# The S5 stage of a two-layer encoder: other engines for the first tables, another loop order, and output-projection splits moved under the last gate unit

## The chip, the cores and the metric

One core of a Trainium2 chip runs the whole program in one launch. The time is device microseconds, the median of three executions. The engines are TensorE (PE in the profile; PEld is its weight load), VectorE (DVE), ScalarE (ACT), GpSimd (POOL) and SyncE (SP), which here issues all the large transfers. Each runs its own list of instructions in order, and they wait for one another through semaphores.

## What is computed

Two layers on a sequence of 1024 tokens of width 1024, batch 1, in float32. Layer 0 mixes with S5 (the stage that the change touches), layer 1 with HGRN2; after each mixer come a projection, a layer norm, a SwiGLU feed-forward of hidden width 2816 and another layer norm.

```python
def s5_direction(u, lam_re, lam_im, log_step, b_re, b_im, c_re, c_im):
    ...
    lam_dt = lam * step
    lam_bar = jnp.exp(lam_dt)
    b_bar = ((lam_bar - 1.0) / lam)[..., None] * b
    powers = jnp.exp(lam_dt[None] * jnp.arange(1, blk + 1, dtype=f32)[:, None, None])
    ...
        bu = jnp.einsum('lbgh,gph->lbgp', u_blk.astype(jnp.complex64), b_bar)
        _, h_loc = lax.associative_scan(combine, (a_blk, bu), axis=0)
        h_all = h_loc + powers[:, None] * h[None]
        y = jnp.einsum('ghp,lbgp->lbgh', c, h_all).real
    ...

def s5_mixer(x, w_in, lam_re, lam_im, log_step, b_re, b_im, c_re, c_im, d_skip, w_glu, b_glu, w_out):
    u = x @ w_in
    ...
    y = (y_fw + y_bw) + d_skip * u
    y = jax.nn.gelu(y)
    y = y * jax.nn.sigmoid(y @ w_glu + b_glu)
    return y @ w_out
```

There are 64 groups of 16 channels with 64 complex states each, scanned over the sequence in both directions.

## The kernel before

All of S5 is in `s5_gate_block`: five instruction lists written out by hand, one per engine. The channels are worked in 8 blocks of 128 (the index `n`, `KT` = 8). Each float32 operand of a large product is split in two rounded parts (`hi` by ScalarE, `lo` = rest by VectorE or GpSimd), and a product is three TensorE instructions. The sequence is cut in chunks of `L` = 8 tokens.

**The front.** x is transposed in 16 tiles (`turn_x`, `split_x`). Meanwhile VectorE works out the tables: `tables_to_first_power` (lambda-bar; 11 small instructions after ScalarE's tanh and sin), `tables_to_input_factors`, then the input factors `b_bar` of block 0, then `make_bl` (12 products of 128x512, of which GpSimd takes the 6 of the backward side), then `scan_factors` (six levels of `k.mu`, ended by the semaphore `mu`), then `scan(0)`.

**Block n.** `inputs(n)` on TensorE makes u = x @ w_in for 128 channels, 48 instructions in two halves; it needs `w_hi` and `w_lo`, of which there is one buffer each: ScalarE's `split_w(n)` waits until `inputs(n-1)` is through (`u_done`), GpSimd's `split_w(n)` follows it (`w_lo_done`). `make_bl` fills `bl`; `turn_bl` transposes it (16 instructions) and ScalarE's `keep_min` puts it in `s5_min`; `start_state` multiplies u of each chunk by it; `scan` on VectorE runs over the chunks in PSUM; `keep_state` on ScalarE copies the result. `make_cl` (backward side, GpSimd, 6 products) and `make_cl_in_psum` (forward side, VectorE, 12 smaller ones, from a copy of c that ScalarE's `place_c` puts in PSUM) fill `cl` for the output. `make_kern` makes the kernel inside a chunk; ScalarE copies it, `turned_diagonal` on VectorE adds the skip term, and SyncE regroups it by way of DRAM (`place_toeplitz`). `within_chunks` and `across_chunks` then give y, `keep_y` copies it, and SyncE regroups it by way of DRAM.

**The loop** (n = 1 to 7) on the three engines that matter:

- TensorE: `start_state(n)`, `make_kern(n)`, `within_chunks(n-1)`, `across_chunks(n-1)`, `inputs(n+2)` (only n = 2 to 5), `turn_bl(n+1)`.
- ScalarE: `keep_kern_rows(n)`, `keep_y(n-1)`, `keep_u(n+2)`, `split_w(n+3)`, `place_b`, `keep_min(n+1)`, `place_c(n+1)`, `keep_state(n)`, `gelu(n-1)`.
- GpSimd: `make_cl(n)`, `ins(n+1)` (its `b_bar` and its `bl`), `split_w(n+3)` (n up to 4). Each item waits for what it reads and overwrites.

SyncE runs one list too: `regroup_u(n+1)`, `put_y` and `regroup_y(n-1)`, then `place_toeplitz(n)`; so the kernel of block 1 is placed only after y of block 0 has been stored.

**The end of S5.** Eight gate units (y @ w_glu, 48 instructions each, two halves) end in `gates(n)`: a sigmoid on ScalarE and a multiplication on VectorE (`mixed`). Then `project_and_feed` begins as a new block of instructions: the gated rows and the pieces of w_out are split on ScalarE and VectorE, and TensorE begins the output projection when row 0 and quarter 0 of piece 0 are split.

Of the kernel before, what the change touches and what calls it, by code (L numbers as in the profile page):

```python
# [78 lines left out]

class Core:  # L80
# [34 lines left out]
    def sb(self, name, shape, dt=F32, keep=False):  # L115
        if dt == F32R:
            with self.nc.sbuf_tensor(name + "_plain", shape, F32) as self.plain[name]:
                pass
        return (self.ctx if keep else self.areas[-1]).enter_context(self.nc.sbuf_tensor(name, shape, dt))
# [42 lines left out]
PIECE = 2 * D  # L162
SLOTS = 6


def out_projection_block(k, tag, w, residual, natural, gamma=None, beta=None):

    k.projection = (tag, w, residual, natural)
    if not natural:
        k.first, k.hi0, k.lo0 = (k.sb("w_" + n, [P, PIECE], F32R, keep=True) for n in ("raw0", "hi0", "lo0"))  # L170
# [24 lines left out]
def project_and_feed(k, gamma_out, beta_out, first_weights=(), spill=None, out=None):  # L195
# [29 lines left out]
    PAIRS = NT // 2  # L225
    turns = out is None
# [179 lines left out]
    with nc.Block() as block:  # L406
        @block.sync
        def _(s):
# [54 lines left out]
            s.wait_ge(S["w_lo"], 2 * KT)  # L463
# [71 lines left out]
        def _(t):  # L535
# [156 lines left out]
            for n, (dh, kh) in enumerate(PIECES):  # L692
                if n < 2:
                    for at in range(4):
                        t.wait_ge(S["x_lo"], at + 1)
                        t.wait_ge(S["w_lo"], 4 * n + at + 1)
                        for tt in range(4):
                            project(n, at, tt, 2 * tt + dh)
                else:
                    t.wait_ge(S["x_lo"], KT)  # L700
                    t.wait_ge(S["w_lo"], 4 * n + 4)
# [45 lines left out]
        def _(a):  # L747
# [3 lines left out]
            def split_piece(n, at):  # L751
# [3 lines left out]
                if n == 2 and at == 0:  # L755
# [94 lines left out]
            for n in range(2):  # L850
                for at in range(4):
                    if not natural or n and at == 3:
                        split_x(4 * n + at)
                    if n or not natural:
                        split_piece(n, at)
# [74 lines left out]
        def _(v):  # L930
            chain = Steps(S["chain"])

            def split_x(kk):
                if not natural:
                    v.wait_ge(S["x_hi"], kk + 1)
# [5 lines left out]
            def split_piece(n, at):  # L941
                dh, kh = PIECES[n]
                if n or not natural:
                    v.wait_ge(S["w_hi"], 4 * n + at + 1 - (4 if natural else 0))
# [202 lines left out]
            for n in range(2):  # L1147
                for at in range(4):
                    split_x(4 * n + at)
                    split_piece(n, at)  # L1150
# [203 lines left out]
def s5_gate_block(k, w_glu):  # L1354
# [5 lines left out]

    w_raw = k.sb("s5_w_raw", [P, KT, P])
# [4 lines left out]
    b_pair = k.sb("s5_b_pair", [P, 2, DP, 2, GRP])  # L1366
# [41 lines left out]
        "u_kept", "bar", "bl", "bl_bw", "pow", "cl", "b_placed", "kern_done", "kern_rows_kept",  # L1408
        "kern_rows_done", "kern_out", "toep_placed", "u_out", "u_grouped", "bl_turned", "min_kept", "in_done",
        "scan", "pads", "state_kept", "toep_done", "out_done", "y_kept", "y_out", "y_ungrouped", "y_done", "mu", "cl_fw", "c_placed", "diag",  # L1410
        "y_hi", "y_lo", "y_lo_last", "glu_loaded0", "glu_loaded1", "glu_hi0", "glu_hi1", "glu_lo0", "glu_lo1", "unit", "gated", "mixed", "early")}
# [7 lines left out]
    FIRST_POWER = LAM_READY + GJ - 1 + 11  # L1419
    POW = 18  # L1420
# [41 lines left out]
    def make_bl(e, n, sides=(0, 1), sem="bl", temp=None):  # L1462
        link = Steps(S[sem], n and n * BL - BL // 2)
        for d in sides:
# [5 lines left out]
            product_steps(link, e, b, pows, [bl[:, q, dps] for q in range(2)],  # L1470
                          gen_t[:, :, 0:L, :] if temp is None else temp)
# [13 lines left out]
    def make_cl_in_psum(e, n):  # L1485
        link = Steps(S["cl_fw"], (n - 1) * CLF)
# [7 lines left out]
    with nc.Block() as block:  # L1494
        @block.sync
        def _(s):
# [139 lines left out]
            s.wait_ge(S["early"], 16)  # L1636

        @block.tensor
        def _(t):
# [50 lines left out]
            def turn_bl(n):  # L1690
                if n >= 1:
                    t.wait_ge(S["bl"], (n + 1) * BL - BL // 2)
# [4 lines left out]
                else:  # L1697
                    t.wait_ge(S["kern_rows_done"], n)
                    t.wait_ge(S["cl_fw"], (n - 1) * CLF)
                for m in range(4):  # L1700
                    if n == 0:
                        t.wait_ge(S["bl" if m < 2 else "bl_bw"], BL // 4 * (m % 2 + 1))
# [92 lines left out]
            inputs(2, (0, 1))  # L1795
            start_state(1)
            make_kern(0)
            inputs(3, (0, 1))
            for n in range(1, KT):
# [4 lines left out]
                across_chunks(n - 1)  # L1804
                if 2 <= n < KT - 2:
                    inputs(n + 2, (0, 1))
                if n < KT - 1:
                    turn_bl(n + 1)

            def gate_part(n, halves, kks):  # L1810
                for half in halves:
# [9 lines left out]
                    if kks[-1] == KT - 1:  # L1821
                        ins.then_inc(S["unit"], 1)

# [1207 lines left out]
```

## Time and profile before

| | us |
|---|---|
| median of 3 executions | 2645.22 (2644.72 to 2647.85) |
| the profiled execution, its own time | 2644.07 |
| its span in the trace | 2642.3 |
| S5 stage (last gate multiplication begins) | 407.43 |

TensorE is busy 94% of the span, but in the S5 stage less: in the windows of 50 us from 100 to 350 it was busy 31.0, 41.8, 41.9, 32.7 and 45.4. The rest of the program (feed-forwards, HGRN2) has no line in the change, apart from counts. Times in rows are microseconds from the start of the span, "idle before" is how long the engine stood before an instruction, and the name behind the arrow is what ended that.

### The profile page before, as it was taken

To read this page: it belongs to the slowest core of one execution; us is meant where nothing else is said; L and a number is where in the kernel's file an instruction comes from. 1 tells how busy PE (TensorE), PEld (TensorE's weight loads), DVE (VectorE), ACT (ScalarE), POOL (GpSimd) and SP (SyncE) were. 2 spreads that over 40 slices of the span, in tenths; PEclk is the share of its full clock that TensorE was granted. 3 is DMA by queue.
4 is the path that set the end of the run, shared out by engine and by line. 5 is a ranking of instruction groups with operands and counts; after the bars stand their busy time and mean duration, and the time that the engine had idled before them with its cause. 6 is when DMAs were issued, how large, how long until landed. Compare 5 with 4: busy or idle time off the path is not lost. (4 is left out here: it accounts for less than half of the span.)

```text
span 2642.3 us, 39850 instructions
## 1 busy us (share of the span) xinstructions
PE 2488.7 (94%) x12860; PEld 2085.5 (79%) x12860; DVE 1920.4 (73%) x3122; ACT 900.0 (34%) x1455; POOL 727.2 (28%) x557
## 2 busy tenths in 40 slices
PE   7678799999999999999999999998799999999997
PEld 6567687878888878887888888887677888887886
DVE  8879826777877758884667666676586777785887
ACT  3223324243333335523322223223124333333641
POOL 6768810243333310001111111112024333331000
PEclk9888899999999999999999999999899999999999
DMA  4143314056677678722010110100404667667863
GB/s 146 56 118 105 97 56 160 13 150 214 192 222 214 204 264 281 233 102 63 25 41 24 40 32 24 40 24 16 159 8 135 203 207 220 209 200 259 296 207 130
DMA packets 442288, 355.97 MB, mean 135 GB/s; under 512 B 30272, under 2 KB 376512, under 8 KB 438464
## 3 DMA queue, kind: packets, MB, share of 16 engines
q1 hardware_dynamic: 442176, 354.52, 42.9%
q8 instruction: 65, 1.06, 0.2%
q14 instruction: 47, 0.39, 0.0%
HBM read 296.31 MB, written 58.13 MB: 134 GB/s over the span
## 5 line engine op out<-in xcount | busy, mean ns | idle before, releaser
L2514 PE MATMUL ps<-aT_hi,w_hi 128*128 128x512 f32 x624 | 250.7, 402 | 3.8 <-DVE hg_q_raw L2793 2.0
L2464 POOL TENSOR_TENSOR w_lo<-w_raw_plain,w_hi 128x1024 fp32r<-128x1024 f32 x38 | 90.9, 2401 | 575.3 <-ACT w_hi L62 575.3
L2514 PE MATMUL ps<-aT_hi,w_lo 128*128 128x512 f32 x624 | 245.2, 393 | 0.0
L2514 PE MATMUL ps<-aT_lo,w_hi 128*128 128x512 f32 x624 | 243.8, 391 | 0.0
L616 PE MATMUL ps<-aT_hi,hgo_w_sets 128*128 128x512 f32 x640 | 203.0, 393 | 0.0
L616 PE MATMUL ps<-aT_hi,s5o_w_sets 128*128 128x512 f32 x640 | 202.7, 393 | 0.0
L1284 POOL TENSOR_TENSOR s5o_w_sets_plain<-s5o_w_sets_plain 128x512 f32<-128x512 f32 x80 | 109.9, 1374 | 216.7 <-DMA s5o_w_sets_plain<-in_ffn_w_in_dram 216.7
L1284 POOL TENSOR_TENSOR hgo_w_sets_plain<-hgo_w_sets_plain 128x512 f32<-128x512 f32 x80 | 110.6, 1383 | 212.8 <-DMA hgo_w_sets_plain<-in_ffn_w_in_dram 212.8
L616 PEld LDWEIGHTS ps<-aT_hi,hgo_w_sets 128*128 128x128 f32 x640 | 120.4, 188 | 26.4
L616 PEld LDWEIGHTS ps<-aT_hi,s5o_w_sets 128*128 128x128 f32 x640 | 120.2, 188 | 26.3
L2514 PEld LDWEIGHTS ps<-aT_hi,w_hi 128*128 128x128 f32 x624 | 117.5, 188 | 26.9 <-DVE hg_q_raw L2793 2.4
L2514 PEld LDWEIGHTS ps<-aT_hi,w_lo 128*128 128x128 f32 x624 | 117.1, 188 | 25.5
L2514 PEld LDWEIGHTS ps<-aT_lo,w_hi 128*128 128x128 f32 x624 | 117.5, 188 | 23.6
L666 PE MATMUL ps<-aT_hi 128*128 128x512 f32 x576 | 133.0, 390 | 0.0
L62 ACT ACTIVATE s5o_w_sets<-s5o_w_sets_plain 128x512 fp32r<-128x512 f32 (+1 forms) x153 | 101.7, 682 | 90.1 <-POOL s5o_w_sets_plain L1284 53.0
L2554 PE MATMUL ps<-hg_q_decayed,hg_k_used 128*128 128x128 f32 x896 | 121.3, 291 | 11.0 <-DVE hg_q_decayed L2859 11.0
L62 ACT ACTIVATE hgo_w_sets<-hgo_w_sets_plain 128x512 fp32r<-128x512 f32 (+1 forms) x153 | 101.4, 682 | 88.2 <-POOL hgo_w_sets_plain L1284 52.4
L2554 PEld LDWEIGHTS ps<-hg_q_decayed,hg_k_used 128*128 128x128 f32 x896 | 117.2, 197 | 16.9 <-DVE hg_q_decayed L2859 12.4
L666 PEld LDWEIGHTS ps<-aT_hi 128*128 128x128 f32 x576 | 108.1, 188 | 22.9
L616 PE MATMUL ps<-aT_lo,s5o_w_sets 128*128 128x512 f32 x320 | 124.4, 389 | 0.0
L616 PE MATMUL ps<-aT_lo,hgo_w_sets 128*128 128x512 f32 x320 | 124.3, 389 | 0.0
L2859 DVE TENSOR_TENSOR hg_q_decayed<-hg_q_decayed,hg_gate_totals 128x512 f32<-128x512 f32 x96 | 76.2, 835 | 65.2 <-PE ps L2554 65.2
(445 smaller groups left out, 6246.9 us busy)
## 6 DMA issues: line engine op xcount, KB each, us to landing
s5o_w_sets_plain<-in_ffn_w_in_dram SPq DMA_DIRECT2D x168, 256.0 KB, 3.2
hgo_w_sets_plain<-in_ffn_w_in_dram SPq DMA_DIRECT2D x168, 256.0 KB, 3.3
w_raw_plain<-in_hg_w_in_dram SPq DMA_DIRECT2D x40, 512.0 KB, 3.9
aT_hi_plain<-in_ffn_w_out_dram SPq DMA_DIRECT2D x64, 256.0 KB, 4.6
s5o_w_sets_plain<-in_ffn_w_in_dram SPq DMA_DIRECT2D x96, 128.0 KB, 2.7
hgo_w_sets_plain<-in_ffn_w_in_dram SPq DMA_DIRECT2D x96, 128.0 KB, 2.8
s5o_hidden<-s5o_home_plain SPq DMA_DIRECT2D x11, 1024.0 KB, 7.0
hgo_hidden<-hgo_home_plain SPq DMA_DIRECT2D x11, 1024.0 KB, 6.8
```

The lines of the kernel that those rows point to most:

```text
L62: return eng.activation(hi, src, ACT.Copy)
L616: ins = t.matmul(ps[:, 4 * second + to, :], w[:, kk, :], x_sets[x][xs][:, kk, :], start=(kk == 0 and m == 0), stop=(kk == 3 and m == 2))
L666: ins = t.matmul(ps[:, out_bank(p, tt), :], x[:, rows], w, start=(j == 0 and m == 0), stop=(j == LAST and m == 2))
L1284: g.tensor_tensor(other, one, other, PRODUCTS[r][2]).then_inc(S["set_sum"], 1)
L2464: g.tensor_tensor(w_lo[b][:, :, :], w_raw[b][:, :, :], w_hi[b][:, :, :].bitcast(F32), ALU.subtract).then_inc(E[f"w_lo_done{b}"], 1)
L2514: ins = t.matmul(ps[:, half, :], w[b][:, kk, :], x[:, kk, cols], start=(kk == 0 and q == 0), stop=(kk == KT - 1 and q == 2))
L2554: ins = t.matmul(bank_rows(2 + 2 * (lv % 2))[:, c, :], k_used[lv % 2][:, c * HC:(c + 1) * HC], q_used(lv, c), start=True, stop=True)
L2859: ins = v.tensor_tensor(qs, qs, bc(pair(d, lv, d), 2, [P, T // (2 << lv), 1 << lv]), ALU.mult)
```

## The change

- **First tables.** VectorE keeps 4 of the 11 instructions (`tables_to_inverse`) and waits for the tanh alone; the other 7 become 8 on GpSimd (`first_power`) ahead of `later_powers`. `make_bl` of block 0 is all VectorE's. GpSimd then waits for `mu`, so that it runs beside neither that nor `scan_factors`, and only then does `split_w(1)` and `ins(1)`. The forward `cl` of block 0 moves from GpSimd to VectorE (`make_cl_in_psum(0)`, behind `scan(0)`).
- **Before the loop.** `start_state(1)` moves between the halves of `inputs(2)`; on ScalarE `keep_state(0)` stands before the second half's copy.
- **The loop.** On TensorE `turn_bl(n+1)` comes before `inputs(n+2)`; on ScalarE `keep_u(n+2)` and `split_w(n+3)` follow `place_c(n+1)`. On VectorE `turned_diagonal(n)` comes right behind the first level of the scan. GpSimd's order in the loop is as before.
- **The end.** The last gate unit runs by contraction block, both halves of a block together. Under it ScalarE and VectorE split piece 0 of w_out and, as TensorE lets go of each row (`row_free`), rows 0 to 3 of y; the output projection no longer splits or awaits these. `w_raw0` and `w_hi0` are placed on tables that S5 has finished with.

```diff
             def turn_bl(n):
                 if n >= 1:
-                    t.wait_ge(S["bl"], (n + 1) * BL - BL // 2)
+                    t.wait_ge(S["bl"], (n + 1) * BL)
...
             def make_kern(n):
-                t.wait_ge(S["cl"], (n + 2) * CLS)
-                t.wait_ge(S["cl_fw"], (n or 1) * CLF if n < KT - 1 else (n - 1) * CLF + CLS)
+                t.wait_ge(S["cl"], (n + 1) * CLS)
+                t.wait_ge(S["cl_fw"], ((n or 1) + 1) * CLF if n < KT - 1 else n * CLF + CLS)
...
             turn_bl(1)
-            inputs(2, (0, 1))
+            inputs(2, (0,))
             start_state(1)
+            inputs(2, (1,))
             make_kern(0)
             inputs(3, (0, 1))
...
                 within_chunks(n - 1)
                 across_chunks(n - 1)
+                if n < KT - 1:
+                    turn_bl(n + 1)
                 if 2 <= n < KT - 2:
                     inputs(n + 2, (0, 1))
-                if n < KT - 1:
-                    turn_bl(n + 1)
...
+                else:
+                    t.wait_ge(S["gated"], 2 * (n - 4) + 2)
+                    for kk in range(KT):
+                        gate_part(n, (0, 1), (kk,))
...
             for n in range(KT):
+                if n == KT - 2:
+                    a.wait_ge(S["early"], 16)
+                    a.wait_ge(S["out_done"], KT)
+                    for at in range(4):
+                        split_hi(a, in_four(k.first)[:, at, :], in_four(k.early)[:, at, :]).then_inc(S["next_w_hi"], 1)
+                if n == KT - 1:
+                    for kk in range(FIRST_ROWS):
+                        a.wait_ge(S["row_free"], kk + 1)
+                        a.wait_ge(S["mixed"], 2 * (kk + 1))
+                        split_hi(a, in_tokens(k.aT_hi[:, kk, :]), in_chunks(row(kk))).then_inc(S["next_x_hi"], 1)
                 gates(n)
...
             make_b_bar(v, 0)
             v.wait_ge(S["pow"], POW)
-            make_bl(v, 0, (0,))
+            make_bl(v, 0)
             scan_factors()
...
             scan(0)
+            v.wait_ge(S["c_placed"], 1)
+            make_cl_in_psum(v, 0)
...
             split_w(0)
-            g.wait_ge(S["tab"], FIRST_POWER)
+            first_power()
             later_powers()
-            g.wait_ge(S["bar"], BAR)
-            make_bl(g, 0, (1,), "bl_bw", cl[0][:, 0, 0:PR, 0:L, :])
+            g.wait_ge(S["mu"], 1)
             split_w(1)
-            g.wait_ge(S["bl"], BL // 2)
             ins(1)
+            g.wait_ge(S["c_kept"], 8)
+            make_cl(g, 0, 1, S["cl"], 0)
             split_w(2)
-            g.wait_ge(S["mu"], 1)
-            g.wait_ge(S["c_kept"], 8)
-            make_cl(g, 0, 0, S["cl"], 0)
-            make_cl(g, 0, 1, S["cl"], CLS)
             split_w(3)
```

Where it moves instructions: TensorE in the loop, pass n = 2 before. L1746 is `start_state`, L1722 `make_kern`, L1762 `within_chunks`, L1775 `across_chunks`, L1667 `inputs` (48 rows of which the first two are here), L1707 `turn_bl`.

```order
L1722 MATMUL ps<-s_cl_plain,s_b_pair 32x128 x16
L1762 MATMUL ps<-s_u_grp,s_pw_in 128x128 x8
L1775 MATMUL ps<-s_state,s_cl 128x128 x32
L1667 MATMUL ps<-aT_hi,s_w_hi 128x512
L1667 MATMUL ps<-aT_lo,s_w_hi 128x512
```

The same place of the changed kernel; L1748, L1788, L1801, L1733 and L1693 are the lines 1722, 1762, 1775, 1707 and 1667 of before.

```order
L1748 MATMUL ps<-s_cl_plain,s_b_pair 32x128 x16
L1788 MATMUL ps<-s_u_grp,s_pw_in 128x128 x8
L1801 MATMUL ps<-s_state,s_cl 128x128 x32
L1733 MATMUL ps<-ident,s_bl 128x128 x16
L1693 MATMUL ps<-aT_hi,s_w_hi 128x512
```

The transposes of `bl` now stand ahead of the input product of the same pass; nothing was added.

ScalarE, pass n = 4 before: `keep_y`, `keep_u`, `split_w`, `place_b`, `keep_min`, `place_c`, `keep_state`.

```order
L1917 ACTIVATE h<-ps 128x4x128 x2
L1866 ACTIVATE h<-ps 128x512 x2
L62 ACTIVATE s_w_hi<-s_w_raw 128x1024
L1875 ACTIVATE s_b_pair<-s_b_bar 64x16x16 x2
L1890 ACTIVATE s_min_plain<-ps 128x512 x4
L1881 ACTIVATE ps<-s_c_all 128x128
L1910 ACTIVATE s_state<-ps 128x4x128 x4
```

The same pass of the changed kernel:

```order
L1953 ACTIVATE h<-ps 128x4x128 x2
L1909 ACTIVATE s_b_pair<-s_b_bar 64x16x16 x2
L1926 ACTIVATE s_min_plain<-ps 128x512 x4
L1917 ACTIVATE ps<-s_c_all 128x128
L1900 ACTIVATE h<-ps 128x512 x2
L62 ACTIVATE s_w_hi<-s_w_raw 128x1024
L1946 ACTIVATE s_state<-ps 128x4x128 x4
```

The copy of u and the split of the next weights now stand behind `place_c`, just ahead of `keep_state`.

GpSimd, the end of one pass and the begin of the next in the changed kernel (the same items in the same order as before): `bl` of block 3, the split for block 5, `cl` of block 3.

```order
L1474 TENSOR_TENSOR s_gen_t<-s_b_bar,s_pw 128x4x128
L1476 TENSOR_TENSOR s_bl<-s_bl,s_gen_t 128x512
L2314 TENSOR_TENSOR s_w_lo<-s_w_raw,s_w_hi 128x1024
L1472 TENSOR_TENSOR s_cl<-s_c_all,s_pw 128x576
L1474 TENSOR_TENSOR s_gen_t<-s_c_all,s_pw 128x576
```

The split stands between `bl` of one pass and `cl` of the next, as it did.

## Rows read from the trace of the kernel before

**Rows 1.** The page's part 1: busy time, share of span, instructions.
```profile
PE 2488.7 (94%) x12860; PEld 2085.5 (79%) x12860; DVE 1920.4 (73%) x3122; ACT 900.0 (34%) x1455; POOL 727.2 (28%) x557
```

**Rows 2.** Waits of TensorE, 0 to 420: total us, times, longest.
```profile
PE ps L1746 <- ACT s_state L1910: 26.9, 7, 11.4
PE ps L1818 <- POOL aT_lo L2269: 4.6, 2, 3.6
```

**Rows 3.** Timeline of ScalarE: start, us, line, tiles [idle before <-releaser].
```profile
165.56 0.60 ACT L1866 ACTIVATE h<-ps 128x512 f32<-128x512 f32 x1 [4.91 <-PE ps L1667]
...
228.44 0.60 ACT L1866 ACTIVATE h<-ps 128x512 f32<-128x512 f32 x1 [4.91 <-PE ps L1667]
...
259.65 0.60 ACT L1866 ACTIVATE h<-ps 128x512 f32<-128x512 f32 x1 [4.91 <-PE ps L1667]
...
276.63 1.08 ACT L1917 ACTIVATE h<-ps 128x512 f32<-128x512 f32 x2 [5.33 <-PE ps L1775]
```

**Rows 4.** Timeline of GpSimd, one pass of the loop.
```profile
198.91 2.36 POOL L2259 TENSOR_TENSOR s_w_lo<-s_w_raw,s_w_hi 128x1024 fp32r<-128x1024 f32 x1 [4.87 <-ACT s_w_hi L62]
201.21 1.18 POOL L1446 TENSOR_TENSOR s_cl_plain<-s_c_all,s_pw 128x576 f32<-128x576 f32 x1
...
208.95 0.40 POOL L1446 TENSOR_TENSOR s_b_bar<-s_b_all,s_coef 128x128 f32<-128x128 f32 x1
...
211.71 1.06 POOL L1446 TENSOR_TENSOR s_bl<-s_b_bar,s_pw 128x512 f32<-128x512 f32 x1
...
224.45 1.30 POOL L1450 TENSOR_TENSOR s_bl<-s_bl,s_gen_t 128x512 f32<-128x512 f32 x1
230.13 2.36 POOL L2259 TENSOR_TENSOR s_w_lo<-s_w_raw,s_w_hi 128x1024 fp32r<-128x1024 f32 x1 [4.38 <-ACT s_w_hi L62]
```

**Rows 5.** Timeline of TensorE, two places of the loop.
```profile
217.16 0.47 PE L1667 MATMUL ps<-aT_hi,s_w_hi 128*128 128x512 f32 x1 [1.28 <-ACT h L1917]
...
282.93 3.78 PE L1707 MATMUL ps<-ident,s_bl 128*128 128x128 f32 x16 [6.35 <-issue]
```

**Rows 6.** Timeline of VectorE, the front.
```profile
30.57 0.22 DVE L2097 TENSOR_TENSOR s_cl<-s_cl 128x64 f32<-128x64 f32 x1
...
35.90 0.69 DVE L1446 TENSOR_TENSOR s_bl<-s_b_bar,s_pw 128x512 f32<-128x512 f32 x1
36.51 1.55 DVE L1448 TENSOR_TENSOR s_gen_t<-s_b_bar,s_pw 128x512 f32<-128x512 f32 x1
...
64.56 2.60 DVE L2127 TENSOR_SCALAR s_mu<-s_mu 128x448 f32<-128x448 f32 x1
```

**Rows 7.** Timelines of ScalarE and TensorE, first store of y.
```profile
129.29 1.06 ACT L1917 ACTIVATE h<-ps 128x512 f32<-128x512 f32 x2
...
144.69 2.71 PE L1762 MATMUL ps<-s_u_grp,s_pw_in 128*128 128x128 f32 x11 [8.69 <-DMA s_pw_in<-s_scratch_kern]
```

**Rows 8.** Timelines of VectorE and ScalarE, scan of block 6.
```profile
264.26 0.46 DVE L1446 TENSOR_TENSOR s_cl_plain<-ps,s_pw 128x288 f32<-128x288 f32 x1
...
269.68 0.69 DVE L2159 TENSOR_TENSOR s_scan_t<-ps,s_mu 128x512 f32<-128x512 f32 x1
...
294.50 1.08 ACT L1910 ACTIVATE s_state<-ps 128x512 f32<-128x512 f32 x2 [0.90 <-DVE ps L2167]
```

**Rows 9.** Timeline of GpSimd, first gate weights split.
```profile
296.92 2.38 POOL L2264 TENSOR_TENSOR s_w_lo<-s_w_raw,s_w_hi 128x1024 fp32r<-128x1024 f32 x1
```

**Rows 10.** Timelines of VectorE, ScalarE and TensorE, end of the S5 stage.
```profile
407.43 0.69 DVE L2251 TENSOR_TENSOR h<-h,s_scan_t 128x512 f32<-128x512 f32 x1 [4.80 <-ACT s_scan_t L1950]
...
408.42 2.04 ACT L62 ACTIVATE aT_hi<-h 128x1024 fp32r<-128x1024 f32 x1 [1.02 <-PEq L1494]
...
415.56 2.44 ACT L62 ACTIVATE aT_hi<-h 128x1024 fp32r<-128x1024 f32 x1
...
413.25 0.77 PE L577 MATMUL ps<-w_raw,aT_hi 128*128 128x512 f32 x1 [6.58 <-DVE w_hi L945]
```

**Rows 11.** Windows: us, busy us (x) of PE, PEld, DVE, ACT, POOL, PEclk, DMA.
```profile
282.90:287.00 4.10, 3.78 (x16) 3.06 (x16) 3.83 (x17) 2.05 (x4) 3.94 (x4) 0.56 0.38 112
```

More of the change, by code:

```diff
@@ L169, in out_projection_block @@
     if not natural:
-        k.first, k.hi0, k.lo0 = (k.sb("w_" + n, [P, PIECE], F32R, keep=True) for n in ("raw0", "hi0", "lo0"))
+        k.lo0 = k.sb("w_lo0", [P, PIECE], F32R, keep=True)
         k.raw0 = k.plain["w_raw0"]
@@ L851, in _ @@
                 for at in range(4):
-                    if not natural or n and at == 3:
+                    if (4 * n + at == KT - 1) if natural else (4 * n + at >= ROWS_DONE):
                         split_x(4 * n + at)
-                    if n or not natural:
+                    if n:
                         split_piece(n, at)
@@ L942, in split_piece @@
                 dh, kh = PIECES[n]
-                if n or not natural:
-                    v.wait_ge(S["w_hi"], 4 * n + at + 1 - (4 if natural else 0))
+                if n:
+                    v.wait_ge(S["w_hi"], 4 * n + at + 1 - 4)
                 v.tensor_tensor(in_four(proj_lo[dh][kh])[:, at, :], in_four(raw[n])[:, at, :],
@@ L1359, in s5_gate_block @@
     GA = SG // 2
+    b_pair = k.sb("s5_b_pair", [P, 2, DP, 2, GRP])
+    k.under.close()
+    k.first, k.hi0 = (k.sb("w_" + n, [P, PIECE], F32R, keep=True) for n in ("raw0", "hi0"))
+    k.sb("s5_gap", [P, HALF // 8])
     w_raw = k.sb("s5_w_raw", [P, KT, P])
@@ L1460, in make_b_bar, with make_bl @@
         product_steps(link, e, b, cf, [of(b_bar[:, q, :, :]) for q in range(2)], t)
-    def make_bl(e, n, sides=(0, 1), sem="bl", temp=None):
-        link = Steps(S[sem], n and n * BL - BL // 2)
-        for d in sides:
+    def make_bl(e, n):
+        link = Steps(S["bl"], n * BL)
+        for d in range(2):
             half = [P, PR, L, GRP]
@@ L1469, in make_bl @@
             pows = [bc(asc[:, q, at, L - 1::-1] if d == 0 else asc[:, q, at, 0:L], 3, half) for q in range(2)]
-            product_steps(link, e, b, pows, [bl[:, q, dps] for q in range(2)],
-                          gen_t[:, :, 0:L, :] if temp is None else temp)
+            product_steps(link, e, b, pows, [bl[:, q, dps] for q in range(2)], gen_t[:, :, 0:L, :])
     def powers(n, d, rows_):
@@ L1822, in gate_part @@
                         ins.then_inc(S["unit"], 1)
+                    elif n == KT - 1 and half == 1:
+                        ins.then_inc(S["row_free"], 1)
             t.wait_ge(S["glu_lo0"], 1)
@@ L1981, in _ @@
             keep_min(1)
+            place_c(0)
+            keep_u(2, (0,))
+            keep_state(0)
             place_c(1)
-            keep_u(2)
+            keep_u(2, (1,))
             split_w(3)
-            keep_state(0)
             keep_kern_rows(0)
@@ L2004, in _ @@
                     keep_y(0)
+                if n >= 2 and n + 2 < KT:
+                    keep_u(n + 2)
+                    if n + 3 < KT:
+                        split_w(n + 3)
                 if n == KT - 2:
@@ L2247, in _ @@
             for n in range(KT):
+                if n == KT - 2:
+                    for at in range(4):
+                        v.wait_ge(S["next_w_hi"], at + 1)
+                        v.tensor_tensor(in_four(k.hi0)[:, at, :], in_four(k.early)[:, at, :],
+                                        in_four(k.first)[:, at, :].bitcast(F32), ALU.subtract).then_inc(S["next_lo"], 1)
+                if n == KT - 1:
+                    for kk in range(FIRST_ROWS):
+                        v.wait_ge(S["next_x_hi"], kk + 1)
+                        v.tensor_tensor(in_tokens(k.aT_lo[:, kk, :]), in_chunks(row(kk)),
+                                        in_tokens(k.aT_hi[:, kk, :]).bitcast(F32), ALU.subtract).then_inc(S["next_lo"], 1)
                 for half in range(2):
```

116 lines of the change are left out of this document (72 added, 44 removed).

## Prediction, made before the changed kernel ran

> **What bounds the kernel now.** Read first the busy times: TensorE works 94% of the span [rows 1], so outside the S5 stage nothing can move, and a gain or loss has to come from its idle time in S5. Then the waits of TensorE there [rows 2]: 26.9 us for `keep_state`, that is for VectorE's scans, and 4.6 us for GpSimd's split of y. Then ScalarE's timeline: the second half of `keep_u` begins the moment `inputs` ends, so its rows give the length of a pass. `inputs(4)` ends at 165.56 and `inputs(7)` at 259.65 [rows 3]: three passes in 94.1 us, 31.4 each. Last GpSimd's list [rows 4], which looks harmless: one pass is `split_w` at 198.91, `cl` from 201.21, `b_bar` from 208.95, `bl` from 211.71 until 225.75 (224.45 + 1.30), together 26.8 us, and then it idles 4.38 us until ScalarE has split the next weights. It fits under the 31.4 only because `inputs` runs while `bl` is being made. The reader is to see that these two are what the new loop order puts in series.
>
> **The front.** Three things, followed to the place where the loop takes over.
> First tables: VectorE no longer waits for the sine and has 4 instructions, not 11. I take 3 us off the second half of x's transposes and all that follows them (bounds 0 and 3.5).
> `make_bl(0)`, scan factors: a 128x512 product on VectorE took 0.69 us just before GpSimd's began and 1.55 beside it; a 128x64 product 0.22 alone; the last factor instruction, begun beside GpSimd, 2.60 [rows 6]. GpSimd now stands still until `mu`. So 12 products x 0.7 = 8.4 us instead of the six contended ones, then 6 levels x 4 instructions x 0.22 plus copies and the negation, about 6 us instead of 23. From 32.9 (35.90 less 3): 41.3, then 47.3 for `mu` (bounds 46 and 50), against 67.2 (64.56 + 2.60). So `scan(0)` begins 20 us earlier.
> The Trainium skill (SBUF — State Buffer, Who interferes with whom) has it that a VectorE instruction with two SBUF inputs contends with a GpSimd one that reads SBUF, and the later one is held. The rows above agree; if the slow level were VectorE's own, 12 x 1.5 and 23 us would put `mu` at 74 and the whole result some 26 us later than I forecast.
> But GpSimd has waited too. From 47.3 it needs, by its rows [rows 4], split 2.4, `b_bar` 2.8, `bl` 14.0, `cl` 7.7 and split 2.4: 76.6 before the weights of `inputs(2)` are split. Then, estimated from the rows of the loop: half a product 5.6 and 1.4 for an idle stretch before it; two copies 1.2; `start_state(1)`, paced by four more, 5; the other half 5.6: 95.4. ScalarE's copy and split 1.7, GpSimd's split 2.4, `cl(1)` 7.7, `b_bar` 2.8, `bl(2)` 14.0: 124. `turn_bl(2)` 3.8, then `place_c` and `keep_y(0)`: 129.8, where before it ended at 130.35 (129.29 + 1.06) [rows 7]. From there the order on SyncE is unchanged: y is stored, then the kernel placed, and 14.3 us later `within_chunks(1)` starts [rows 7], so at 144.1; the chunk products, some 8.3 at the low clock, make it 152.4; with `turn_bl(3)` 3.8 and `inputs(4)` 11.3 it is 167.5. Before: 165.56. The 20 us of `scan(0)` have gone in GpSimd's later start: **+1.9 us** (bounds -2 and +5).
>
> **The loop.** Moving `turn_bl(n+1)` ahead of `inputs(n+2)` closes a ring. `turn_bl` needs `bl` from GpSimd; `inputs` stands behind it on TensorE; ScalarE may overwrite the one `w_hi` buffer only when `inputs` is through; GpSimd's `split_w(n+3)` waits for that, and `cl`, `b_bar` and the next `bl` stand behind it in its list. Its price, all from rows: GpSimd 26.8 [rows 4]; 16 transposes 3.8 and 48 products from 217.16 to 228.44 = 11.3 [rows 3, 5]; ScalarE's copy and split until GpSimd starts, 228.44 to 230.13, 1.7 [rows 3, 4]. Together 43.6 us. From `inputs(4)` to `inputs(7)` the ring is closed three times (splits for blocks 5, 6, 7): 3 x 43.6 - 94.1 = **+36.7 us** (bounds: +35 if the transposes need no more than 3.2; +53 if every input product runs half its length at the low clock, 3 x 5.6 more; I take the low end, since the 3.8 was read with the granted clock at 0.56 of full, the low level of 1.2 GHz for most of it, and is paid already [rows 11]). What else the order brings, `place_c` without waiting behind `inputs`, and `turned_diagonal` early, shortens waits that are no longer last. VectorE needs 24.8 + 5.4 us in a pass (scan 6 from 269.68 to 294.47, the forward `cl` before it from 264.26) [rows 8] and now idles 13.
> The Trainium skill (Perfetto Trace Analysis, Optimization Strategy) says that the same gap coming back in each pass can mean that there is no buffer for the next tile. Before, no gap here was of that kind; by that rule the new one would be, since `w_hi` is single.
>
> **Out of the loop.** Before, `inputs(7)` ended at 259.6 and scan 6 34.9 us later, for it was queued behind scan 5 [rows 3, 8]. Now scan 5 is long done: copy, `keep_state(5)`, half of `start_state(6)`, 3 us, and 24.8: 27.8. **-7.0 us** (bounds -5 and -8). GpSimd's last two `cl` (2 x 7.7) begin when `across_chunks(5)` ends. Before, that was 17.0 us after `inputs(7)` (276.63 - 259.65) [rows 3]; without the transposes between, 3.8 and a wait of some 1.5, it is 11.7, so `split_glu(0)` starts 27.1 after it; before it was 296.92 - 259.65 = 37.3 [rows 9], 10.2 more. The stage's tail is 3.2 us nearer to its splits of y than to its scans, and 4.6 us were waited for them [rows 2]: **-3.2 us** (bounds 0 and -4.6).
>
> **The last gate unit and the output projection.** Before, TensorE stood 6.58 us [rows 10] between the stages: sigmoid, multiplication, then row 0 and a quarter piece split. Now it can begin when the new block does. Under the last unit (11 us on TensorE) ScalarE has four row splits of 2.0 to 2.4 and VectorE four of the same size behind them; the first can begin 1.4 us into the unit. The last ends at 1.4 + 4 x 2.3 + 2.6 = 13.2, then two multiplications 1.4: 14.6 against 12.5 before, so the stage ends 2 us later; the block's first instruction comes at 408.42 before, hence TensorE at 410.5 instead of 413.25. With a little less time at the low clock: **-3.5 us** (bounds -5 and +1). The next pieces' splits are done before TensorE reaches them, 11 us on. The four quarter splits of w_out fall in gaps of 4.80 us on ScalarE.
>
> **Sum.** 1.9 + 36.7 - 7.0 - 3.2 - 3.5 = +24.9 us. The profiled execution took 2644.07, 1.8 more than its span of 2642.3, and the median of the runs is 1.2 above it; I put the difference on the median: 2645.2 + 24.9 = 2670.
>
> **The rivals.**
> The ring doesn't bind and VectorE does. Then each pass is 30.2 us, and the early `scan(0)` reaches the end: scan 6 would begin at 47.5 + 6 x 30.2 + 5.4 (the added `cl` of block 0) = 234.1 instead of 269.68 [rows 8], 35.6 us earlier; with the projection's 3.5: 2606. It decides from the point at which `bl` is ready when `across_chunks` ends. For it speaks that VectorE was busy nearly all of a pass before; against it that each link of the ring is a wait in the code. Chance 0.05.
> The ring binds, but the front's gain arrives at `inputs(4)` and the clock costs nothing, some 20 us less than my sum: 2650, still within 0.2% of before. GpSimd's 29 us behind `mu` speak against it. Chance 0.03.
> The ring binds and TensorE, which now idles 10 us twice in a pass, runs the products behind at the low clock: up to 3 x 5.6 more, and 2 in the front: 2689. The stretch of the 16 transposes shows 0.56 of full speed on the mean, so the clock was already rising within it, and little is left for the products. Chance 0.07.
> The splits under the last unit hold up the stage by 5 us more: 2675, inside the range.
>
> **The numbers.** The forecast has 0.85. The ends of its own terms would reach from 2653 to 2700, which they do not do together; 2660 to 2681 leaves out both outer rivals and the far tails, about 2 in 10. About 0.2%, 5 us, is what a measurement of this kernel can tell. Faster 0.05, same 0.03, slower 0.92.
>
> **What would show it.** Right: in the trace of after `keep_u`'s second halves for blocks 4 to 7 some 43 to 44 us apart; `turn_bl` idle about 10 us before each and released by GpSimd's `bl`; `mu` at 46 to 50 and `scan(0)` right behind; GpSimd idle 17 us before each split; TensorE idle below 4 us ahead of the projection. Wrong: passes of 30 to 32 us, or `turn_bl` released by anything but `bl`.

## The result, and the profile after

| | median us | lowest to highest | profiled execution, its span |
|---|---|---|---|
| before | 2645.06 | 2644.72 to 2647.85 (4 runs) | 2644.07, 2642.3 |
| after | 2668.97 | 2666.09 to 2671.44 (4 runs) | 2669.25, 2667.5 |

The changed kernel is slower: 1.009 times the time before (95% interval 1.0076 to 1.0103), 23.9 us by the medians and 25.2 us by the spans. The forecast was 2670. Two executions lie far outside all others (10923 us in run 2, 3514 us for the kernel before beside runs 9 and 10) and are left out of every median below.

Part 1 of the page of after, engine by engine: busy time, share of the span, instructions.

```profile
PE 2495.0 (94%) x12860; PEld 2089.1 (78%) x12860; DVE 1914.2 (72%) x3133; ACT 900.2 (34%) x1456; POOL 714.1 (27%) x553
```

Against [rows 1] TensorE is busy 6.3 us longer with the same 12860 instructions; the other 19 us are idle time. Of the 6.3 us, 6.0 lie in the S5 stage, where the mean granted clock fell from 0.89 to 0.87. Nothing is computed more, so the loss has to be read from waits. TensorE's waits from 0 to 450 us (us in total, times, longest):

```profile
PE ps L1733 <- POOL s_bl L1476: 32.8, 5, 8.3
PE ps L1772 <- ACT s_state L1946: 22.3, 7, 10.6
PE ps L1693 <- POOL s_w_lo L2314: 11.0, 3, 6.3
PE ps L1748 <- POOL s_cl L1476: 9.9, 2, 5.8
PE ps L1788 <- DMA s_pw_in<-s_scratch_kern: 7.5, 1, 7.5
```

L1733 is `turn_bl`, L1748 `make_kern`. In [rows 2] the first place belonged to `keep_state`, that is to VectorE's scans. Now `turn_bl` waits longest, and for GpSimd. ScalarE's timeline shows how far apart the passes lie: `keep_u`'s second halves for blocks 4 to 7 (start, us, line, tiles, idle before and releaser), to be laid beside [rows 3]:

```profile
167.05 0.60 ACT L1900 ACTIVATE h<-ps 128x512 f32<-128x512 f32 x1 [4.90 <-PE ps L1693]
...
210.40 0.60 ACT L1900 ACTIVATE h<-ps 128x512 f32<-128x512 f32 x1 [4.90 <-PE ps L1693]
...
254.21 0.60 ACT L1900 ACTIVATE h<-ps 128x512 f32<-128x512 f32 x1 [4.90 <-PE ps L1693]
...
298.30 0.60 ACT L1900 ACTIVATE h<-ps 128x512 f32<-128x512 f32 x1 [4.89 <-PE ps L1693]
```

The passes take 43.35, 43.81 and 44.09 us; before it was 31.4. The first of them, link by link, in the timelines of GpSimd, TensorE, ScalarE and again GpSimd:

```profile
168.73 2.36 POOL L2314 TENSOR_TENSOR s_w_lo<-s_w_raw,s_w_hi 128x1024 fp32r<-128x1024 f32 x1 [17.09 <-ACT s_w_hi L62]
...
194.14 1.26 POOL L1476 TENSOR_TENSOR s_bl<-s_bl,s_gen_t 128x512 f32<-128x512 f32 x1
```

```profile
195.46 3.83 PE L1733 MATMUL ps<-ident,s_bl 128*128 128x128 f32 x16 [8.26 <-POOL s_bl L1476]
198.94 0.65 PE L1693 MATMUL ps<-aT_hi,s_w_hi 128*128 128x512 f32 x1
```

```profile
210.89 1.05 ACT L62 ACTIVATE s_w_hi<-s_w_raw 128x1024 fp32r<-128x1024 f32 x1
```

```profile
212.08 2.35 POOL L2314 TENSOR_TENSOR s_w_lo<-s_w_raw,s_w_hi 128x1024 fp32r<-128x1024 f32 x1 [16.67 <-ACT s_w_hi L62]
```

From split to split it is 212.08 - 168.73 = 43.35: GpSimd's list until 195.40 (26.7), the transposes until the product starts at 198.94 (3.5), the product until 210.40 (11.5), copy and split on ScalarE (1.7). No link overlaps another. That is what a closed chain (a ring) looks like: each engine idles in each pass, and each waits for the one before it.

At the end of the stage, the timelines of ScalarE, VectorE and TensorE; `aT_hi` and `aT_lo` x4 are the splits of y's rows under the last gate unit, behind the last sigmoid of the unit before it at 424.84, to be laid beside [rows 10] and this sigmoid of before:

```profile
395.72 0.69 ACT L1950 ACTIVATE s_scan_t<-ps,glu_col 128x512 f32<-128x512 f32 x1 [4.80 <-PE ps L1818]
```

After:

```profile
424.84 0.69 ACT L1986 ACTIVATE s_scan_t<-ps,glu_col 128x512 f32<-128x512 f32 x1 [4.80 <-PE ps L1845]
426.21 8.71 ACT L62 ACTIVATE aT_hi<-h 128x1024 fp32r<-128x1024 f32 x4 [0.68 <-PE ps L1845]
435.14 1.38 ACT L1986 ACTIVATE s_scan_t<-ps,glu_col 128x512 f32<-128x512 f32 x2 [0.22 <-PE ps L1845]
```

```profile
428.51 8.73 DVE L2301 TENSOR_TENSOR aT_lo<-h,aT_hi 128x1024 fp32r<-128x1024 f32 x4 [2.25 <-ACT aT_hi L62]
```

```profile
438.76 0.77 PE L586 MATMUL ps<-w_raw,aT_hi 128*128 128x512 f32 x1 [2.96 <-PEq L1519]
```

TensorE stands 2.96 us between the stages instead of 6.58. The projection starts at 438.76, 25.5 us later than before, and that is the whole loss: from there to the end of the span it is 2228.7 us, and before 2229.0.

### The profile page after: what moved, and what is told of

The parts are those of the page before. It is cut to its first block and busy times, and to the rows that moved or that the text cites. A ratio compares the mean times of both kernels' runs of the same rounds, so it can differ in the third digit from the quotient of the medians.

```text
span 2667.5 us, 39858 instructions
## 1 busy us (share of the span) xinstructions
PE 2495.0 (94%) x12860; PEld 2089.1 (78%) x12860; DVE 1914.2 (72%) x3133; ACT 900.2 (34%) x1456; POOL 714.1 (27%) x553
## 3 DMA queue, kind: packets, MB, share of 16 engines
q8 instruction: 65, 1.06, 0.2%
## 5 line engine op out<-in xcount | busy, mean ns | idle before, releaser
L2584 PEld LDWEIGHTS ps<-aT_hi,w_hi 128*128 128x128 f32 x624 | 117.8, 189 | 27.8 <-DVE hg_q_raw L2863 2.9
L2584 PEld LDWEIGHTS ps<-aT_hi,w_lo 128*128 128x128 f32 x624 | 117.5, 188 | 25.6
```

Of the source, the lines that this page charges most:

```text
L2584: ins = t.matmul(ps[:, half, :], w[b][:, kk, :], x[:, kk, cols], start=(kk == 0 and q == 0), stop=(kk == KT - 1 and q == 2))
```

## Experiments

Throughout, the comparison is with the kernel before on the same chip (medians of 2644.70 to 2645.13), and a ratio is to that.

**1. Loop orders taken back.** In the changed kernel TensorE's and ScalarE's loop orders are those of before; the front and the end stay changed. TensorE's part of the edit:

```diff
...
                 across_chunks(n - 1)
-                if n < KT - 1:
-                    turn_bl(n + 1)
                 if 2 <= n < KT - 2:
                     inputs(n + 2, (0, 1))
+                if n < KT - 1:
+                    turn_bl(n + 1)
...
```

The other part puts ScalarE's `keep_u(n+2)` and `split_w(n+3)` back ahead of `place_b`.

> The changed kernel with the two loop orders of before (TensorE: inputs(n+2) ahead of turn_bl(n+1); ScalarE: keep_u and split_w ahead of place_b), all else as changed. Ring theory: the passes between inputs(4) and inputs(7) fall from 43.8 us back to 31.2 to 31.7; start_state(2) begins at 131.3, 0.3 later than before, so the S5 stage ends as before or 0.4 later, and the split output projection gives 3.6: 2642 us (2639 to 2645). Rival, the front costs the time (GpSimd stands still until mu and VectorE has one more forward cl): 2660 or more.

Measured: 2637.26 us, ratio 0.9974 (0.9963 to 0.9986), faster than before. ScalarE, `keep_u` of blocks 4 and 7:

```profile
164.05 0.60 ACT L1900 ACTIVATE h<-ps 128x512 f32<-128x512 f32 x1 [4.90 <-PE ps L1693]
...
258.04 0.60 ACT L1900 ACTIVATE h<-ps 128x512 f32<-128x512 f32 x1 [4.90 <-PE ps L1693]
```

Three passes in 93.99, 31.3 each. So 31.7 us of the result come with the loop orders, and the other parts together are a gain. It was 5 us better than expected, below the range's low end of 2639: in the trace `inputs(4)` ended 1.5 us earlier than before, where the loop's start was expected 0.3 later, and run 9 shows how little that can be laid to the edit.

**2. Loop orders alone.** The same blocks moved the other way in the kernel before, nothing else. TensorE's part (ScalarE's moves with it):

```diff
...
                 across_chunks(n - 1)
+                if n < KT - 1:
+                    turn_bl(n + 1)
                 if 2 <= n < KT - 2:
                     inputs(n + 2, (0, 1))
-                if n < KT - 1:
-                    turn_bl(n + 1)
...
```

> The kernel before with the two loop orders alone changed. Ring theory: inputs(4) ends 2.7 us later (16 transposes ahead of it), three passes of 43.6 to 44.0 instead of 31.4 give 37, the scan of block 6 is no longer queued (-6.7), GpSimd's late splits of y are awaited less (-2.8): +30 us, 2675 (2671 to 2680). Rival, the order costs only because GpSimd starts late in the new front: under 2655.

Measured: 2677.87 us (three executions), ratio 1.0124 (1.0099 to 1.0149), 32.9 us slower. Passes: `keep_u` of block 4 and of block 7.

```profile
168.01 0.60 ACT L1866 ACTIVATE h<-ps 128x512 f32<-128x512 f32 x1 [4.90 <-PE ps L1667]
...
300.19 0.60 ACT L1866 ACTIVATE h<-ps 128x512 f32<-128x512 f32 x1 [4.90 <-PE ps L1667]
```

132.2 us, 44.1 each. With run 1 this shows that the orders make the ring, in either surrounding.

**3. The link between ScalarE and GpSimd cut.** The changed kernel, with VectorE making `w_lo` of blocks 5 to 7, so that GpSimd's list waits for no split.

```diff
+                if 5 <= n + 2 < KT:
+                    v.wait_ge(S["w_hi_done"], n + 3)
+                    v.tensor_tensor(w_lo[:, :, :], w_raw[:, :, :], w_hi[:, :, :].bitcast(F32),
+                                    ALU.subtract).then_inc(S["w_lo_done"], 1)
...
-                if n + 3 < KT:
-                    split_w(n + 3)
+                if n == 1:
+                    split_w(4)
```

The first four lines stand at the head of VectorE's pass n, the others in GpSimd's loop.

> The changed kernel, order and all, but the low parts of w_in for blocks 5, 6 and 7 are made by VectorE ahead of its forward cl, not by GpSimd behind bl: one link of the ring is cut and the order kept. Ring theory: passes bound by VectorE, 25 + 5.4 + 1.4 = 31.9 us, not 43.8; then 2643 us (2639 to 2648). Rival, the order is slow by itself (ScalarE's keep_state behind keep_u, TensorE waiting for the transposes): passes stay above 38 and the time above 2655.

Measured: 2637.76 us, ratio 0.9974 (0.9964 to 0.9983). ScalarE, `keep_u` of blocks 4 and 7:

```profile
166.94 0.60 ACT L1900 ACTIVATE h<-ps 128x512 f32<-128x512 f32 x1 [4.90 <-PE ps L1693]
...
262.51 0.60 ACT L1900 ACTIVATE h<-ps 128x512 f32<-128x512 f32 x1 [4.90 <-PE ps L1693]
```

31.9 us a pass on the mean (31.4, 29.8 and 34.4), with TensorE's new order in place; the time is 1.2 us below the expected range. The order alone does no harm; it does through this one link.

**4. Less work in the ring.** The changed kernel, with GpSimd's `cl` and `b_bar` of the next pass made ahead of the split, so that only `bl` stands between the split and `turn_bl`.

```diff
...
                 if n + 1 < KT:
-                    ins(n + 1)
+                    g.wait_ge(S["bl_turned"], 4 * (n + 1))
+                    make_bl(g, n + 1)
+                if n + 1 < KT:
+                    g.wait_ge(S["out_done"], n)
+                    make_cl(g, n + 1, 1, S["cl"], (n + 1) * CLS)
...
+                if n + 2 < KT:
+                    g.wait_ge(S["b_placed"], 2 * (n + 2))
+                    make_b_bar(g, n + 2)
                 if n + 3 < KT:
                     split_w(n + 3)
```

> The changed kernel, but on GpSimd the next block's cl and b_bar (10.5 us) stand ahead of split_w, so they run while TensorE transposes and multiplies; bl alone stays behind the split. Ring theory: each pass shortens by just these 10.5 us, 43.8 to 33.3; with 3 passes -31 us: 2638 us (2635 to 2643). Rival, VectorE or ScalarE takes over before that: passes above 35, 2645 or more.

Measured: 2638.43 us, ratio 0.9973 (0.9964 to 0.9983). ScalarE:

```profile
168.02 0.60 ACT L1900 ACTIVATE h<-ps 128x512 f32<-128x512 f32 x1 [4.90 <-PE ps L1693]
...
269.92 0.60 ACT L1900 ACTIVATE h<-ps 128x512 f32<-128x512 f32 x1 [4.90 <-PE ps L1693]
```

34.0 us a pass: 9.8 less than in after, against 10.5 us taken out of the ring. The ring is priced link by link.

**5. The end taken back.** The changed kernel, but the last unit and the projection's first splits as before (two of the edit's places are here).

```diff
-                if n < KT - 1:
-                    for half in range(2):
-                        t.wait_ge(S["gated"], 2 * (n - 4) + half + 1)
-                        gate_part(n, (half,), range(KT))
-                else:
-                    t.wait_ge(S["gated"], 2 * (n - 4) + 2)
-                    for kk in range(KT):
-                        gate_part(n, (0, 1), (kk,))
+                for half in range(2):
+                    t.wait_ge(S["gated"], 2 * (n - 4) + half + 1)
+                    gate_part(n, (half,), range(KT))
...
-                if n == KT - 1:
-                    for kk in range(FIRST_ROWS):
-                        a.wait_ge(S["row_free"], kk + 1)
-                        a.wait_ge(S["mixed"], 2 * (kk + 1))
-                        split_hi(a, in_tokens(k.aT_hi[:, kk, :]), in_chunks(row(kk))).then_inc(S["next_x_hi"], 1)
```

> The changed kernel with the parts at its end taken back: the last gate unit keeps its old order, and the first rows and the first weight piece of the output projection are split behind it as before the change. Front and loop orders stay as changed. If the end is worth what the sum gave it (3.5 us; the trace after shows 3.6 from the last front stage to the projection's start), this takes 2669 + 3.6 = 2672.6 us (2671 to 2675). Rival: the gain at that place is given back inside the projection, and this takes 2669 us within 1.

Measured: 2674.1 us, ratio 1.0117 (1.0099 to 1.0134). TensorE, first instruction of the projection:

```profile
441.85 0.77 PE L584 MATMUL ps<-w_raw,aT_hi 128*128 128x512 f32 x1 [6.58 <-DVE w_hi L952]
```

The 6.58 us are back, and the projection starts 3.1 us later than in after; by the medians the end is worth 5.1 us. The two ratio intervals overlap by a little, so the size is good to a few us only. From the end of `inputs(7)` (297.89 here) to the projection it is 143.96 us against 140.46 in after: 3.5.

**6. GpSimd doesn't stand still.** The changed kernel, but GpSimd waits for VectorE's `mu` behind its first products, not ahead of them; ahead of them it waits only for VectorE's products of block 0 (`bl`).

```diff
-            g.wait_ge(S["mu"], 1)
             split_w(1)
+            g.wait_ge(S["bl"], BL)
             ins(1)
+            g.wait_ge(S["mu"], 1)
             g.wait_ge(S["c_kept"], 8)
```

> The changed kernel, but GpSimd makes the first block's products as soon as the table of l is there, instead of first waiting for VectorE to finish with the front. If the wait is what lets VectorE be done with the factors at 47.7 us, its operations now stand beside GpSimd's again (1.55 us instead of 0.69 for the products, 1.1 instead of 0.22 for the small ones): the factors come at 62 to 67 us, the first scan's end, the start state of block 1 and inputs(4) come about 6 us later, and the total is 2675 us (2670 to 2682). Rival: GpSimd was the late one, its start some 10 us earlier reaches the loop, and the total is 2662 us or less.

Measured: 2669.16 us, ratio 1.0095 (1.008 to 1.0111): the time of after within 0.2 us, and both expectations missed. VectorE, scan factors and the scan's start, in this run:

```profile
47.66 1.11 DVE L2170 TENSOR_TENSOR s_mu<-s_mu,s_cl 128x64 f32<-128x64 f32 x1
48.81 0.99 DVE L2164 TENSOR_TENSOR s_mu<-s_mu 128x64 f32<-128x64 f32 x1
...
62.02 0.42 DVE L2172 TENSOR_SCALAR s_mu<-s_mu 128x448 f32<-128x448 f32 x1
62.51 0.67 DVE L2204 TENSOR_TENSOR s_scan_t<-ps,s_mu 128x512 f32<-128x512 f32 x1
```

and in after:

```profile
43.12 0.23 DVE L2170 TENSOR_TENSOR s_mu<-s_mu,s_cl 128x64 f32<-128x64 f32 x1
43.38 0.23 DVE L2164 TENSOR_TENSOR s_mu<-s_mu 128x64 f32<-128x64 f32 x1
...
47.32 0.42 DVE L2172 TENSOR_SCALAR s_mu<-s_mu 128x448 f32<-128x448 f32 x1
47.80 0.67 DVE L2204 TENSOR_TENSOR s_scan_t<-ps,s_mu 128x512 f32<-128x512 f32 x1
```

The wait does what it is for: small products take 0.23 instead of 1.0 to 1.1 us, and the scan starts 14.7 us earlier. It buys nothing. GpSimd's next split, which paces the front, in after and then in this run:

```profile
98.09 2.35 POOL L2314 TENSOR_TENSOR s_w_lo<-s_w_raw,s_w_hi 128x1024 fp32r<-128x1024 f32 x1 [20.98 <-ACT s_w_hi L62]
```

```profile
98.23 2.37 POOL L2314 TENSOR_TENSOR s_w_lo<-s_w_raw,s_w_hi 128x1024 fp32r<-128x1024 f32 x1 [25.60 <-ACT s_w_hi L62]
```

In after `inputs(2)` waits for GpSimd's late split (until 77.16), here `start_state(1)` waits for the late scan (4.82 us, until 85.86); both ways the block is through at 96.5. I had let the later scan reach `start_state(1)` 6 us late; it had 14.6 us of slack (in after it was over at 72.4, and `start_state(1)` came at 87.0), and this run spends just that. The expectation had left that slack out, and the rival had left out that TensorE meets the late scan next.

**7. The ring opened by GpSimd's list.** The changed kernel; GpSimd's splits for blocks 5 to 7 stand one pass later in its list, each right behind the `bl` whose transposes TensorE does ahead of the input product.

```diff
                 if n + 1 < KT:
                     ins(n + 1)
-                if n + 3 < KT:
-                    split_w(n + 3)
+                if n == 1:
+                    split_w(4)
+                if 5 <= n + 2 < KT:
+                    split_w(n + 2)
```

> The changed kernel with only GpSimd's list changed: the split of weight block 5 and the later ones stands behind the pass's products instead of ahead of them, and one pass earlier in the count, so that it is made a whole pass before TensorE asks for it. If the 43.8 us of a pass are the closed chain (split, product of the inputs, kernel columns, turned products, next split), it is open now and VectorE's 30 us bind: passes of about 30.4 us, total 2630 us (2626 to 2636). Rival: another resource holds the passes (ScalarE's evictions in their new order, or the PSUM banks), and the total stays above 2655 us.

(The text on record has the shift the wrong way round: the split comes a pass later, not earlier. Its 2.4 us lie under the 3.8 us of transposes, so it is ready as TensorE asks.)

Measured, inside the range: 2633.21 us, ratio 0.9959 (0.9945 to 0.9972), 35.8 us below after with not one instruction more or less. VectorE, first instruction of the scans of blocks 4, 5 and 6:

```profile
203.74 0.69 DVE L2204 TENSOR_TENSOR s_scan_t<-ps,s_mu 128x512 f32<-128x512 f32 x1
...
233.97 0.69 DVE L2204 TENSOR_TENSOR s_scan_t<-ps,s_mu 128x512 f32<-128x512 f32 x1
...
264.21 0.69 DVE L2204 TENSOR_TENSOR s_scan_t<-ps,s_mu 128x512 f32<-128x512 f32 x1
```

30.2 us apart, with no idle time in front of any of them: VectorE binds now. TensorE is even a little faster (`keep_u` of block 7 at 255.60, 29.2 us a pass), and hands its lead back behind the loop, where `start_state(7)` waits 12.05 us for the scan.

**8. The Toeplitz block earlier.** As run 7, and SyncE places the kernel of block 1 ahead of fetching y of block 0.

```diff
-                elif n >= 1:
+                elif n >= 2:
                     ungroup_y(n - 1)
                 if n < KT - 1:
                     place_toeplitz(n)
+                if n == 1:
+                    ungroup_y(0)
```

> As the run before this one, and besides SyncE places the Toeplitz block of block 1 before it fetches the ungrouped y of block 0, on which TensorE waited 7.5 us in within(1). If that wait stands on the path at the front, inputs(4) ends about 7 us earlier and the total is 2624 us (2619 to 2632). Rival: the start state of the next block ends last there anyway, and the total is that of the run before within 2 us.

Measured: 2629.62 us, ratio 0.9946 (0.9932 to 0.9959), the fastest kernel here. It is inside the range, but not by the expected way, and 3.6 us below run 7, more than the rival allowed. TensorE at the place in question (L1790 is `within_chunks`, L1735 `turn_bl`):

```profile
137.89 1.27 PE L1790 MATMUL ps<-s_u_grp,s_pw_in 128*128 128x128 f32 x9
...
150.97 3.83 PE L1735 MATMUL ps<-ident,s_bl 128*128 128x128 f32 x16 [7.25 <-POOL s_bl L1476]
```

`within_chunks(1)` starts with no wait at 137.89, but the transposes behind it now wait for `bl(3)` on GpSimd, so `inputs(4)` ends at 166.7 instead of 167.9, and not 7 us earlier. The DMA wait had GpSimd right behind it. In the old order, where `inputs(4)` does not stand behind `bl(3)`, the same edit does bring it forward: to 156.50 in run 10 from 164.05 in run 1. Of the 3.6 us between the medians the traces show 1.2 at `inputs(4)` and 3.1 at the projection's start (400.17 against 403.25); the 1.9 between are not explained by the edit.

**9. The front alone.** The changed kernel with both the loop orders (run 1) and the end (run 5) taken back.

> The changed kernel with both the loop orders of TensorE and ScalarE and the parts at its end as before the change: what is left is the rebuilt front (VectorE's products of block 0 and GpSimd's wait). Theory: the three parts add up, so this lies above the run with only the orders taken back (2637.3 us) by what the end is worth (3.6 us by the trace, up to 5 us by the run without it): 2641.5 us (2639 to 2644). Rival: the front alone brings nothing and this takes 2645 us, as before the change.

Measured: 2644.69 us, ratio 0.9999 (0.999 to 1.0007). That is above the theory's range and the rival's number: the front brings nothing.

```profile
166.12 0.60 ACT L1886 ACTIVATE h<-ps 128x512 f32<-128x512 f32 x1 [4.90 <-PE ps L1686]
...
413.69 0.76 PE L584 MATMUL ps<-w_raw,aT_hi 128*128 128x512 f32 x1 [6.58 <-DVE w_hi L952]
```

`inputs(4)` ends 0.6 us later than before and the projection starts 0.4 us later. By these medians the end gives 7.4 us, where run 5 had 5.1. The traces don't bear that size out: from `inputs(7)` to the projection it is 153.80 us here and 150.05 in run 1, 3.75 apart, which agrees with the 3.5 of run 5. Another 2.1 us lie ahead of `inputs(4)` (164.05 in run 1, 166.12 here), where both kernels have the same instruction lists, and 2.9 behind the projection's start.

**10. The ring open, the loop orders of before.** As run 8, with TensorE's and ScalarE's orders of before.

> The run with GpSimd's later splits and the earlier Toeplitz block (2629.6 us), but with TensorE's and ScalarE's loop orders as before the change. Theory: with the chain open VectorE's 30.3 us of a pass bind in either order, so the orders no longer matter: 2629.6 us (2627 to 2633), scans starting 30.3 us apart. Rival: TensorE's order costs or gives something by itself (a wait of its own in front of the turned products or of the scan's start state), and the total is 4 us or more away from that.

Measured: 2638.84 us, ratio 0.9979 (0.997 to 0.9989), 9.2 us behind run 8; the theory that the orders don't matter once the chain is open fell. TensorE at the start of `inputs(6)` and `inputs(7)`, and GpSimd between:

```profile
213.96 0.50 PE L1695 MATMUL ps<-aT_hi,s_w_hi 128*128 128x512 f32 x1 [3.94 <-POOL s_w_lo L2313]
...
248.45 0.50 PE L1695 MATMUL ps<-aT_hi,s_w_hi 128*128 128x512 f32 x1 [4.12 <-POOL s_w_lo L2313]
```

```profile
229.28 0.40 POOL L1472 TENSOR_TENSOR s_b_bar<-s_b_all,s_coef 128x128 f32<-128x128 f32 x1 [7.72 <-ACT s_b_pair L1911]
```

It is another ring. In the old order ScalarE places b behind `keep_u` and the split, so GpSimd's `b_bar` waits for the input product (until 229.28), `bl` follows, and the late split behind `bl` is what the next input product waits for: 34.5 us from one product to the next. Each of the two loop orders has one place of GpSimd's split that suits it, and in each the other place closes a ring. The old order with its own place of the split and the earlier Toeplitz block was not run.

## Why the prediction was right, step by step

- **Front, +1.9.** `mu` was done at 47.74 (forecast 47.3), the scan began at 47.80, `bl(2)` ended at 124.9 (124), `inputs(4)` at 167.05 (167.5): +1.5. The points on the way were met to about 1 us, in one place by two errors that offset: the first half of `inputs(2)` took 8.6 us, not 7.0, and `start_state(1)` 3.7, not 5. Run 9 confirms that nothing of the scan's 19 us arrives. What the prediction did not see is that GpSimd's start was not the only cover: run 6 starts GpSimd 5.4 us sooner and the front is no shorter.
- **Ring, +36.7.** Measured 298.30 - 167.05 = 131.25 for three passes against 94.1: +37.2. GpSimd 26.7 (26.8), transposes 3.5 (3.8), product 11.5 to 12.2 (11.3), handover 1.7 (1.7). The three products took 1.7 us more than forecast together, and the transposes 0.9 less; TensorE idled 8.3, 8.3 and 7.5 us before them, not 10. The surplus in the products is the low clock. The windows of the first transposes and of the last of the three products (us, busy us of the engines, granted clock, DMA share):

```profile
195.40:199.30 3.90, 3.84 (x17) 3.47 (x18) 3.80 (x7) 1.79 (x3) 0.01 (x1) 0.50 0.39 99
...
286.10:298.30 12.20, 12.16 (x50) 9.61 (x48) 6.89 (x15) 1.61 (x5) 11.49 (x15) 0.92 0.25 65
```

  The transposes run at 0.50 of full, the 1.2 GHz level, behind 8 us of idling. The first of the three products has 0.98 and the last 0.92; the last one's first instructions still take 0.63 us each, its later ones 0.39. So the choice of the low end, with the cost of the clock inside the transposes, was right, and the rival with 3 x 5.6 us lost. Runs 1 to 4 and 7 show the ring from five sides: orders back, orders alone, one link cut, one link shortened, list turned.
- **Out of the loop, -7.0.** `inputs(7)` ended at 298.3 and the last state of scan 6 was kept from 326.43: 28.1 us (27.8), against 34.9 before. -6.7.
- **GpSimd's y splits, -3.2.** `split_glu(0)` at 325.55 is 27.25 behind `inputs(7)` (27.1). Of the 4.6 us in [rows 2], 1.5 are left on GpSimd, and 2.0 have gone to VectorE's half of the same splits, which no step had. Up to the end of the gates that is -2.8.
- **End, -3.5.** Four row splits on each engine, 8.7 us (9.2), TensorE idle 2.96. From the last sigmoid of the unit before (424.84, before 395.72) to the projection it is 13.9 us instead of 17.5: -3.6. The way there was not quite the forecast one: the last gate multiplication ends 1.2 us later after that sigmoid than before, not 2, and the 0.7 us that the forecast gave to the low clock can't be read apart, so some of the fit is luck. By medians the same part is worth 5.1 (run 5) to 7.4 us (run 1 against run 9), but both pairs hold time from places that the edit doesn't touch, so a larger size is not shown.
- **Sum.** +1.5 + 37.2 - 6.7 - 2.8 - 3.6 = +25.6 against a span longer by 25.2. The terms are not the three parts of the change: the loop's three (26.5 together) begin at `inputs(4)`, but the transposes of block 3, which the new order puts ahead of it, are inside the front's +1.9. Run 2 has `inputs(4)` 2.4 us later than before (168.01 against 165.56), and after has it 3.0 later than run 1. With that the forecast prices the loop orders at 29 to 29.5 us. Measured at the projection's start they cost 28.2 (run 5 against run 9), 30.7 (after against run 1) and 30.0 (run 2); by the medians 29.4, 31.7 and 32.9, each good to some 5 us. So the size of the ring holds, and the front without its transposes is about 1 us of gain in the forecast and 0.4 us of loss in run 9.
- **What is open.** From the projection's start to the end the traces have from 2224.9 us (run 8) to 2232.9 (run 2), at a mean granted clock of 0.99 in each. The four kernels with the old end have 2227.7 to 2232.9, the eight with the new end 2224.9 to 2228.7. Some of the end's gain may therefore lie inside the projection, which has fewer splits to do; with one trace of each kernel that is not shown, and what else sets this time is open.
- **The rivals.** VectorE's 30.2 us a pass do exist: they bind as soon as the ring is open (run 7), where the rival had them. It was given 0.05 on the ground that each link was a wait in the code; that was the right ground. By the rule of the Trainium skill (Perfetto Trace Analysis, Optimization Strategy) a gap that returns in each pass, on the engine that should be saturated, can mean that there is no buffer for the next tile. The trace of after agrees with it as a symptom: TensorE idles 8.26, 8.27 and 7.50 us before the transposes, and GpSimd 17.09, 16.67 and 17.15 before its splits (the first of these was 16.85 before the change too). Run 7 removes the gaps before the transposes and the splits without a buffer. The Trainium skill's rule on contention (SBUF — State Buffer, Who interferes with whom) agrees with run 6: 0.23 against 1.0 to 1.1 us for the same product, with only VectorE's side held.

## What to carry to other kernels

Before two blocks of one engine change places, follow every single-buffered operand round: who may overwrite it, who is queued behind that one, and whether its result feeds what now stands ahead. If the way closes, the pass is the sum of the links and no longer the longest engine, and the page's busy shares, nearly unchanged, hardly tell. The cure can be one line in a third engine's list, but it suits only one order of the others; move both together.

## What the runs showed beyond that

- Beside a product of GpSimd, VectorE's 128x64 product took 0.99 to 1.32 us (run 6) and alone 0.22 to 0.23 (after); GpSimd's own 128x512 product took 1.06 either way, and VectorE's scan instructions, which read PSUM, 0.69 beside GpSimd as well as alone. Taking that contention out moved the scan by 14.7 us and the kernel by 0.2.
- Three parts that were measured alone and together add up only to a few us: front 0.0, orders +32.9, end -7.4 or -5.1 make +25.5 to +27.8; together they are +23.9.
